# Long convolution by even and odd times, in an encoder trunk on one core

## The reference

```
x = x + W_out( sig(g_attn) * P_attn(MLA(n1(x))) + sig(g_hy) * P_hy(Hyena2(n1(x))) )
x = x + ExpertChoiceSwiGLU(n2(x))
```

```
h = (sin(fr2*(sin(fr1*(feats@w1+b1))@w2+b2)) @ w3) * exp(-tau*|deltas|);  h = h / sum|h|
z = parts[0]
for n in range(2):
    z = parts[n+1] * (irfft(rfft(z, 2L) * rfft(h, 2L))[L//2 : L//2+L] + z * skip[n])
```

## Time and profile before

| | us |
|---|---|
| median of 3 runs | 2067.41 |
| lowest and highest | 2064.19, 2067.5 |
| the profiled execution, whole | 2062.56 |
| its span | 2060.6 |
| TensorE busy | 1597.2 (78%) |
| VectorE busy | 509.9 (25%) |
| ScalarE busy | 290.6 (14%) |
| GpSimd busy | 45.7 (2%) |
| mean granted TensorE clock | 0.895 |

### The profile page before, as it was taken

One profiled execution on the slowest core, in us unless ns is written; L12 is line 12 of the kernel. 1 busy time (PEld: TensorE's weight loads), 2 busy tenths in 40 slices (PEclk: granted clock), 3 DMA queues, 4 the chain that ended last, 5 costly groups with the idle time before them and its releaser, 6 DMA issues.

```text
span 2060.6 us, 22212 instructions
## 1 busy us (share of the span) xinstructions
PE 1597.2 (78%) x9564; PEld 888.9 (43%) x9564; DVE 509.9 (25%) x1063; ACT 290.6 (14%) x602; POOL 45.7 (2%) x24
## 2 busy tenths in 40 slices
PE   8999999966665674675799999997766666666657
PEld 5687678532222231222257866884322222222222
DVE  2554541121110120111136445402111011111101
ACT  2243200110000000000032332002000000000000
POOL 0300000000000000000002000000000000000000
PEclk9999999988797797788899999999888887878979
DMA  7522033689999999999965220427899999999997
GB/s 290 211 96 82 1 151 138 250 337 430 433 433 435 429 434 428 434 438 431 417 215 225 82 82 1 204 85 322 341 429 437 430 432 435 432 434 434 432 431 325
DMA packets 24369, 644.22 MB, mean 313 GB/s; under 512 B 2672, under 2 KB 3696, under 8 KB 5104
## 3 DMA queue, kind: packets, MB, share of 16 engines
q1 hardware_dynamic: 23248, 638.73, 73.3%
q10 hardware_dynamic: 1056, 4.53, 0.8%
HBM read 642.21 MB, written 1.05 MB: 312 GB/s over the span
## 4 chain that ended last, share of the span: by engine, by line
DMA 48%; PE 48%; DVE 2%; issue 1%; DVEq 1%; ACT 1%; SPq 0%; ACTq 0%
DMA region<-w_down_dram 46%; PE ps L798 11%; PE ps L460 7%; PE ps L684 5%; PE ps L527 5%; PE ps L709 3%; PE ps L618 2%; PE ps L653 2%; PE ps L643 2%; PE ps L488 2%; DMA qkw<-qkw_dram 2%; PE ps L550 1%; PE ps L505 1%; PE ps L757 1%; PE ps L574 1%; PE ps L542 1%
## 5 line engine op out<-in xcount | busy, mean ns | idle before, releaser
L757 PE MATMUL ps<-ring,uT 128*32 128x384 f32 (+1 forms) x3328 | 335.4, 538 | 263.5 <-DMA ring<-w_gbu_dram 256.1
L757 PEld LDWEIGHTS ps<-ring,uT 128*32 128x32 f32 x3328 | 139.5, 125 | 454.5 <-DMA ring<-w_gbu_dram 275.6
L798 PE MATMUL ps<-region,uT 128*32 128x512 f32 x1408 | 226.7, 765 | 100.5 <-DMA region<-w_down_dram 97.9
L460 PE MATMUL ps<-xnT,ring 128*128 128x256 f32 x768 | 178.3, 380 | 4.3 <-DVE uT L1032 2.6
L1358 DVE TENSOR_TENSOR uT<-uT,ps 128x256 f32<-128x256 f32 x32 | 13.5, 421 | 625.9 <-PE ps L757 625.9
L798 PEld LDWEIGHTS ps<-region,uT 128*32 128x32 f32 x1408 | 56.9, 135 | 248.2 <-issue 160.7
L460 PEld LDWEIGHTS ps<-xnT,ring 128*128 128x128 f32 x768 | 140.6, 190 | 23.9 <-DVE uT L1032 4.4
L813 PE MATMUL ps<-uT 128*128 128x512 f32 x256 | 124.1, 617 | 27.7 <-ACT uT L1016 21.7
L1010 ACT ACT_TABLE_LOAD x32 | 41.1, 1283 | 657.8 <-PE ps L757 657.8
L527 PE MATMUL ps<-xnT,ring 128*128 128x256 f32 x512 | 115.0, 380 | 0.0
L1369 DVE TENSOR_TENSOR x<-x,ps 128x512 f32<-128x512 f32 x128 | 87.9, 687 | 63.0 <-PE ps L813 63.0
(11 more groups left out here) (202 smaller groups left out, 1447.6 us busy)
## 6 DMA issues: line engine op xcount, KB each, us to landing
ring<-w_gbu_dram SPq DMA_DIRECT2D x28, 7040.0 KB, 31.3
region<-w_down_dram SPq DMA_DIRECT2D x28, 5632.0 KB, 32.8
ring<-w_ga_dram SPq DMA_DIRECT2D x16, 4224.0 KB, 28.3
region<-w_ga_dram SPq DMA_DIRECT2D x16, 4224.0 KB, 33.7
ring<-units_dram SPq DMA_DIRECT2D x28, 2048.0 KB, 8.7
region<-w_down_dram SPq DMA_DIRECT2D x8, 2048.0 KB, 16.2
region<-units_dram SPq DMA_DIRECT2D x6, 2048.0 KB, 22.1
ring<-w_gbu_dram SPq DMA_DIRECT2D x2, 4992.0 KB, 15.4
```

The source lines that it names most:

```text
L460: m = mm(bank(b % 2, S), unit8(n)[:, i, j * P:(j + 1) * P], xnT[:, i], start=i == 0, stop=i == DB - 1)
L757: m = mm(bank(b, QW[j], rows=CAP, row0=CAP * j), xs[:, i, q * CAP:(q + 1) * CAP], w[i][:, j * FT:j * FT + QW[j]], start=i == 0, stop=i == ...
L798: m = mm(bank(c, rows=CAP, row0=CAP * j), hT[:, b * P + CAP * j:b * P + CAP * (j + 1)], wd[:, CT * b + j, c * 512:(c + 1) * 512], start=b ...
```

## The change

The transform length of 384 has a symmetry. For a frequency k and its mirror 192 - 1 - k, the sums over even times are the same and the sums over odd times differ in sign (up to conjugation). The kernel after computes sums over even and over odd times at 96 frequencies (`NK`), as 4 products of 512 columns per block and not 6, and forms both halves of the spectrum as even + odd (called A) and even - odd (called B).

- The filter's taps are generated in the order even times, then odd times, by permuting features and decay on the host. ACT copies the odd sums out of PSUM (`odd_filter`), DVE adds and subtracts. The filter in time is double-buffered.
- z is transposed from even and from odd columns. ACT copies the odd sums out (`odd_z`), DVE adds and subtracts, then DVE multiplies the A parts, and GpSimd the B parts (4 operations of 96x512 per block). DVE combines them to real and imaginary parts, and then to even and odd results.
- The inverse is 16 products of 128 columns (the even or the odd times alone) and not 12 of 256; `gate_z` reads them back interleaved.
- All 16 half-pairs of gates are computed before the branch products: two at attention's tail, three in the filter loop, eleven in the long convolution. The loop at line 667 holds branch products only. The units are reordered: gates 7 to 10, branches 11 to 14. Eight sigmoid buffers take the place of four and two.
- The order of the long convolution on TensorE, ACT and DVE is written out step by step. The expert stage is the same, but for a wait of SP for the third merged block ahead of line 329, since sigmoids lie in `ring`.

```diff
                 unit_is_used(11)
                 unit_is_used(12)
+                sp.wait_ge(s["merged_dve"], L * 8 + 3)
                 load_gate_b_up_first(0)
...
+                for it in range(4):
+                    n, c = it // 2, it % 2
+                    hb = [spec[0:NK, n, 2 + f, c * HW:(c + 1) * HW] for f in range(2)]
+                    for f in range(2):
+                        pool.wait_ge(s["b_dve"], L * 8 + 2 * it + f + 1)
+                        nc.gpsimd.tensor_tensor(terms[:, 2 + f], ab[:, 2 + f], hb[f], ALU.mult)
+                        m = nc.gpsimd.tensor_tensor(ab[:, 2 + f], ab[:, 2 + f], hb[1 - f], ALU.mult)
+                    m.then_inc(s["b_pool"], 1)
...
+                def to_spectrum(it):
+                    n, c = it // 2, it % 2
+                    pe.wait_ge(s["z_act"], L * 4 + max(it + 1, 2))
+                    if it == 0:
+                        pe.wait_ge(s["spec_dve"], (L + 1) * 12)
+                    else:
+                        pe.wait_ge(s["b_dve"], L * 8 + 2 * it)
+                    for f in range(2):
+                        for par in range(2):
+                            m = mm(bank(2 * f + par, rows=NK), basis(par, f), z_t[:, c, par], start=True, stop=True)
+                        m.then_inc(s["zf_psum"], 1)
+
+                def from_spectrum(it):
+                    pe.wait_ge(s["yf_dve"], L * 4 + it + 1)
+                    if it >= 1:
+                        pe.wait_ge(s["post_dve"], L * 4 + it - 1 + FREE + 1)
+                    for j in range(4):
+                        for par in range(2):
+                            for f in range(2):
+                                a = C_IF + (2 * par + f) * P
+                                m = mm(bank(5 + j // 2, P, (j % 2) * S + par * P), yf[:, 2 * par + f, j * P:(j + 1) * P],
+                                       cst[0:NK, a:a + P], start=f == 0, stop=f == 1)
+                        if j % 2:
+                            m.then_inc(s["y_psum"], 1)
...
                 filter_time(0)
                 for it in range(4):
                     if it < 3:
                         filter_time(it + 1)
...
+                    filter_spectrum(it)
+                    if it < 3:
+                        more_gates(1)
+                    else:
                         z_transposed(0)
...
+                    filter_sum(it)
+                z_transposed(1)
+                more_gates(1)
                 to_spectrum(0)
...
+                more_gates(2)
+                to_spectrum(1)
+                from_spectrum(0)
+                more_gates(3)
+                z_transposed(2)
+                from_spectrum(1)
+                to_spectrum(2)
+                more_gates(1)
+                z_transposed(3)
+                to_spectrum(3)
+                more_gates(1)
+                from_spectrum(2)
+                more_gates(3)
+                from_spectrum(3)
...
+                z_out(0)
+                z_out(1)
+                sigmoids(2, sg[2], 7)
+                odd_z(0)
+                sigmoids(3, sg[3], 7)
+                odd_z(1)
+                sigmoids(4, sg[4], 7)
+                z_out(2)
+                odd_z(2)
+                sigmoids(5, sg[5], 7)
+                z_out(3)
+                odd_z(3)
+                for i in range(6, DB):
+                    sigmoids(i, sg[i], 7)
...
+                    ha = [spec[0:NK, n, f, c * HW:(c + 1) * HW] for f in range(2)]
                     dve.drain()
...
+                    for f in range(2):
+                        dve.wait_ge(s["odd_act"], L * 8 + 2 * it + f + 1)
+                        even, odd = bank(2 * f, rows=NK), ab[:, 2 + f]
+                        tt(ab[:, f], even, odd, ALU.add)
+                        tt(odd, even, odd, ALU.subtract).then_inc(s["b_dve"], 1)
+                    dve.drain()
+                    for f in range(2):
+                        tt(terms[:, f], ab[:, f], ha[f], ALU.mult)
+                        tt(ab[:, f], ab[:, f], ha[1 - f], ALU.mult)
+                    dve.drain()
+                    tt(terms[:, 0], terms[:, 0], terms[:, 1], ALU.subtract)
+                    tt(ab[:, 0], ab[:, 0], ab[:, 1], ALU.add)
+                    dve.wait_ge(s["b_pool"], L * 4 + it + 1)
+                    tt(terms[:, 2], terms[:, 2], terms[:, 3], ALU.subtract)
+                    dve.drain()
+                    tt(terms[:, 1], ab[:, 2], ab[:, 3], ALU.add).then_inc(s["prod_dve"], 1)
...
+                    for par, op in enumerate((ALU.add, ALU.subtract)):
+                        tt(yf[:, 2 * par], terms[:, 0], terms[:, 2], op)
+                        m = tt(yf[:, 2 * par + 1], ab[:, 0], terms[:, 1], op)
+                    m.then_inc(s["yf_dve"], 1)
...
+                            in_time = uT[:, b0 + r].rearrange("p (m two) -> p m two", two=2)
+                            stt(in_time, in_time, hskip[:, k:k + 1],
+                                bank(5 + jj, S, r * S).rearrange("p (two m) -> p m two", two=2), ALU.mult, ALU.add)
...
                 products(0)
                 spectrum(0)
...
+                products(1)
+                gate_z(0)
+                spectrum(1)
+                gate_z(1)
+                products(2)
+                spectrum(2)
+                products(3)
+                gate_z(2)
+                spectrum(3)
+                gate_z(3)
```

More of the change, by code:

```diff
@@ L596, in z_transposed, with filter_sum @@
+                def filter_sum(it):
+                    pe.wait_ge(s["habs_pool"], L * 4 + it + 1)
+                    if it == 0:
+                        pe.wait_ge(s["sig_act"], L * 8 + 1)
+                    else:
+                        pe.wait_ge(s["spec_dve"], L * 12 + 3 * it)
+                    for j in range(4):
+                        m = mm(bank(2, 1, j), habs[:, j * P:(j + 1) * P], ones, start=True, stop=True)
+                    m.then_inc(s["hsum_psum"], 1)
                 def z_transposed(it):
@@ L607, in _, with more_gates @@
+                def more_gates(count):
+                    for _ in range(count):
+                        next_gates()
                 filter_time(0)
@@ L621, in _ @@
-                    if it == 3:
-                        z_transposed(0)
[L623 to L640, removed]
-                            pe.wait_ge(s["spec_dve"], (L + 1) * 16)
-                        for t in range(SB):
-                            m = mm(bank(2 + f), cst[:, C_F + t * NF + f * P:C_F + t * NF + (f + 1) * P],
-                                   z_t[:, c, t], start=t == 0, stop=t == SB - 1)
-                        m.then_inc(s["zf_psum"], 1)
@@ new lines, in odd_z @@
+                def odd_z(it):
+                    if it >= 1:
+                        act.wait_ge(s["prod_dve"], L * 4 + it)
+                    for f in range(2):
+                        act.wait_ge(s["zf_psum"], L * 8 + 2 * it + f + 1)
+                        af(ab[:, 2 + f], bank(2 * f + 1, rows=NK), ACT.Copy).then_inc(s["odd_act"], 1)
+                abs_h(0)
+                odd_filter(0)
+                abs_h(1)
+                odd_filter(1)
+                sigmoids(1, sg[1], 7)
@@ L1270, in _ @@
                 spectrum(0)
-                for it in range(4):
-                    if it < 3:
-                        products(it + 1)
-                    gate_z(it)
-                    if it < 3:
-                        spectrum(it + 1)
+                products(1)
[8 more added lines that the diff above has]
+                gate_z(3)
                 for i in range(DB):
@@ L1451 @@
     for c in range(2):
-        units += [half(w_in, gate0 + c * HW), half(w_in, gate0 + D + c * HW), half(w_a, c * HW), half(w_h, c * HW)]
+        units += [half(w_in, gate0 + c * HW), half(w_in, gate0 + D + c * HW)]
+    for c in range(2):
+        units += [half(w_a, c * HW), half(w_h, c * HW)]
     units += [half(w_o, 0), half(w_o, HW)]
```

225 lines of the change are left out of this document (91 added, 134 removed).

## The result

| | before | after |
|---|---|---|
| median, six runs each, us | 2065.86 | 2045.34 |
| lowest and highest | 2059.93, 2067.5 | 2040.03, 2047.9 |
| the profiled execution, whole | 2062.56 | 2045.78 |
| its span | 2060.6 | 2043.7 |

The ratio is 0.9902 [0.989, 0.9914]: 20 us faster, 18 to 23. The forecast was 2050.6 in a range of 2030 to 2066.

The account below looks back on a forecast made before the run. TensorE was taken to bound each layer ahead of the HBM-bound expert stage. 10.1 us from the walk less 1.7 for the clock gave 8.4 per layer, 16.8 in all: 2067.4 becomes 2050.6, range 2030 to 2066 (own range 2041 to 2059).

Parts of the forecast that it names:

- The bound: Ahead of the expert stage TensorE bounds each layer; a microsecond off the mixing stage is one off the kernel, per layer.
- TensorE's work: Attention to branch products: 94.8 us, transforms -13.8, inverses -6.6, moved gates +27.6; 101.2 us piece by piece; ceiling 24 us per layer.
- Turn-taking: Long convolution: DVE and GpSimd products exclude each other, 7.1 us per block; gain 10.1 us per layer instead of 18.1.
- Rival 1: Long convolution: GpSimd works beside DVE without turn-taking; gain 18.1 us per layer, 2031.2 us; chance 0.12.
- the walk: Mixing stage: four engine queues stepped in written order with trace durations; 13.6 us of TensorE idle, first branch product at 313.0.
- The clock: Transform part: idles of 2.9 and 2.7 us in doubt; one fall to half clock charged, 1.7 us per layer, leaving 8.4.
- Rival 4: Transform part: five idles each cost a clock fall of 2.9 us; 4.4 us per layer slower, 2076.2 us; chance 0.10.
- Costed at nothing: DVE's stepped PSUM reads of the inverse (4.3 us per layer if doubled), transposes of every second column, unit loads: taken as 0.
- rival 2: Inverse: stepped PSUM reads doubled (4.3) and weight-load-bound products (3.3); gain 0.8 us per layer, 2065.8 us; chance 0.11.
- rival 3: Ahead of the expert stream: the gain is absorbed because expert 0's weights are late; 2067.4 us; chance 0.05.
- The 4.85 us: Whole kernel: offset from the profiled execution, 2062.56 us, to the median, 2067.41, carried from 2045.8 to the forecast 2050.6.
- Half its transform work: Mixing stage: the prediction's question was whether TensorE stays fed when half its transform work goes.

Follow-up runs that it names:

- a quarter: Kernel after with GpSimd multiplying 128 of the 512 columns per operation, the rest of the B products left out: 2030.45 us.
- six operations: Kernel after with one of GpSimd's products done twice per half, six operations per block and not four: 2061.19 us, 0.9987 of before.
- the filler: Kernel after with five unread 256-column products put ahead of the first and the last inverse of each layer: 2045.99 us, 0.9908 of before.
- the run without them there: Kernel after with gates of blocks 4 to 7 back in the branch loop, six half-pairs one each between convolution steps: 2101.75 us, 1.0176 of before.
- two products: Kernel after with the first half's two B products on GpSimd and the second half's two on DVE: 2033.06 us, 0.9845 of before.
- the new order: Kernel after with two B products on GpSimd, one gate half-pair between the first filter products, five before the first inverse: 2028.14 us, 0.982 of before.
- the run with fillers: Kernel after with gates back in the branch loop and unread 256-column products in TensorE's four long idles: 2090.67 us, 1.0124 of before.

## Why the prediction was right, point by point

- **The bound.** Right. What was gained once per layer reached the end: 9 us at the output product in layer 0, 17.6 in layer 1, 16.9 in the span. Between the output product and the first expert's down-weights, layer 0 gave 0.9 back: the gather took 6.46 us at a clock near one half and not 5.33.
- **TensorE's work.** Right. The sum was 101.2 us of work plus idles; a transform took 3.43 to 3.51 us to the next product (forecast 3.44), and an inverse at full clock 3.57 to the next product for 32, forecast 3.55. In the trace of before the nearest row was a gather of the same shape, of which half was at the lower clock. Taking the half at full clock, and not the mean of 5.3, was what made this right.
- **Turn-taking.** Right, by the order of the ends above and by the runs with GpSimd's work taken away, cut to a quarter and raised by half. Rival 1 is out. The term was a little too dear: GpSimd's product counts 1.13 us between ends, where the walk used 1.17, and DVE's 0.55 where it used 0.61. Three of each in turn cost 0.3 us less, about half of what the forecast idles had too much (2.9 and 2.7 forecast, 2.3 and 2.0 logged). Whether this is also why six operations cost less than expected was not tested.
- **The clock.** Right in kind, wrong in count. One fall of 1.7 us was charged, because two idles were in doubt. After both the clock fell, with 1.6 us each on the inverse. But the first one's reached hardly anybody, as DVE was behind by as much: the idle of 1.8 us that the walk had before the second inverse is not in the trace, and with the filler 1.07 of it come back. About one fall is what the path paid, by another reason than the one given; that is luck. Rival 4 is out: the idles of 1.5 us and less were not followed by the lower clock in this trace, and the clock over 198 to 314 us was 0.97.
- **Costed at nothing.** Right. The first gate step on DVE with its stepped reading from PSUM took 0.86 us for two, before 0.87; the eight transposes 0.95 to the next product, 0.08 more than before, so 0.3 us per layer. Both halves of rival 2 are out, and so is rival 3: no load ahead of expert 0 is in the chain.
- **The number.** The sum, made against the profiled execution, gave 2045.8, and the profiled execution of after took 2045.78. The 4.85 us that were added to come from it to the median of three runs are the miss: with six runs the median of before is 2065.86, and that of after lies on its profiled execution. The offset between an execution and the median is a random draw, not a term to be carried over. That sum and execution agree to 0.02 us is luck: the parts do not. Of the forecast's 13.6 us of idle (its nine terms add up to 13.8) the log has 8.8, and about 2 more stand in the log as drains, busy time at the end of a group that waits. There are two falls for one, and the work from each start to the next is about 102 us, not 101.2. Inside the stage the gain is 9.5 us per layer where 8.4 was forecast, and 2.2 of the 19.1 are given back outside it in these two executions.
- **"Half its transform work".** Wrong as a word, without effect on the sum: 4 products for 6, and 32 inverse instructions in 3.55 us for 24 in 5.20, are a third less.

The first gate step's row, to be held against the earlier trace rows:

```profile
265.16 0.86 DVE L1302 SCALAR_TENSOR_TENSOR uT<-uT,small,ps 128x256 f32<-128x256 f32 x2
```

What the forecast did not say, though its numbers held it: at 7.1 us in turn against 4.9 on DVE alone, the GpSimd part is a loss by itself. The gain is the gates as cover, which the run without them there shows most plainly. The runs with two products, with a quarter and with the new order ended 1 to 5 us above what was expected of them. Their traces place most of that in the mixing stage: with two products and with a quarter it gained 1.9 to 2.0 us less per layer than expected, with the new order at least 0.6 less. Which term of those walks was too low stays open. The expert stage's length varied from trace to trace too (from the second to the last issue of a down load 556.6 to 562.5 us in one layer, both in the run with a filler), which medians of several executions should mostly remove.

## What to carry to other kernels

When two engines' operations exclude each other, work moved to the slower one is not taken off the faster one: compare all of it in turn with all of it on one, and give the helper only what falls beside operations that it doesn't block. A cut in TensorE's work inside a chain of dependent steps is worth only as much as there is other work to fill the holes; look first for that, and put it in the longest hole, since an idle of 2 us can cost nearly as much again through the clock, where the work behind it is what the next engine waits for.

## What the runs showed of the hardware

- Nine idles of 1.97 to 2.37 us stand ahead of an inverse in the traces of after, of all B products on DVE and of six operations, both layers counted. Six were followed by the lower clock, with a loss of 1.6 us on the 32 instructions behind; three were not. One length, 2.21 us, is there both ways (5.46 and 3.84 us for the inverse), and 1.98 and 1.97 fell on either side. In this stage idles of 1.46 us and less, with no longer one just ahead of them, were not followed by it, but for the one of 1.29 in layer 1 of the run with fillers (clock 0.55 over the 7 us behind it). So the length of the idle alone doesn't decide. The idle with a fall that I had gone by was 2.87 us long.
- Products with unused results raised the clock over 79 us from 0.78 to 1.00 in layer 0 and from 0.78 to 0.96 in layer 1, for 11 us of the kernel's time.
- GpSimd's product took 1.27 us on 96 partitions, the same as an addition on 128, and 0.45 us for a quarter of the columns: by these two, an estimate, about 0.18 us of it doesn't depend on the size.
- DVE waits even for a GpSimd operation of 0.45 us, and a DVE operation that reads PSUM and one SBUF tensor does not. The Trainium skill, "SBUF — State Buffer", section SBUF: two separate sides, says so of operations with two SBUF inputs; these traces agree, with 1.75 us where such a product runs in 0.68 alone.
